# Gated scan with eight decay blocks: levels built on tokens, a plain product on the diagonal, key products in three pieces

## The reference, cut to what matters

```python
def step(s, inp):                       # one chunk of tokens, one head, one direction
    qc, kc, vc, gc = (t.astype(F32) for t in inp)
    g = jnp.cumsum(gc, axis=2)
    diff = g[:, :, :, None, :] - g[:, :, None, :, :]
    decay = jnp.exp(jnp.where(mask, diff, -jnp.inf))
    att = jnp.einsum('bhik,bhjk,bhijk->bhij', qc, kc, decay)
    o = jnp.einsum('bhij,bhjv->bhiv', att, vc) + jnp.einsum('bhik,bhkv->bhiv', qc * jnp.exp(g), s)
    g_last = g[:, :, -1:, :]
    s = s * jnp.exp(g_last[:, :, 0, :, None]) + jnp.einsum('bhjk,bhjv->bhkv', kc * jnp.exp(g_last - g), vc)
    return s, o
```

## Time and profile before

| | before |
|---|---|
| median of the runs | 3596.71 us |
| profiled execution | 3596.57 us |
| its span on the core | 3594.8 us |
| TensorE busy / share | 3305.3 us / 92% |
| VectorE busy / share | 2276.3 us / 63% |
| GpSimd busy / share | 1000.4 us / 28% |
| L815 key products | 80 of 2660 ns, 212.8 us |
| L1057 predicated copies | 320 of 298 ns |

### The profile page before, as it was taken

How to read it: one execution, slowest core, us unless ns; L and a number is a source line. 1 busy time by engine, 2 the same in 40 slices (tenths; PEclk the granted TensorE clock), 3 DMA queues, 4 the chain that set the end, 5 groups by cost and what they waited for, 6 DMA issues and landing times. The chain is left out here.

```text
span 3594.8 us, 49981 instructions
## 1 busy us (share of the span) xinstructions
PE 3305.3 (92%) x18422; PEld 2780.7 (77%) x18422; DVE 2276.3 (63%) x2915; ACT 993.8 (28%) x1472; POOL 1000.4 (28%) x539
## 2 busy tenths in 40 slices
PE   5989999997979999999997879888988799999998
PEld 3889978886868888888885657777777688888886
DVE  7976078888356666666666256666664556666666
ACT  4111245545141111111112434444442311112111
POOL 1322155552232222222220131212121333333331
PEclk8999999998989999999998879999999899999999
DMA  5557110002211111111100200000002111111111
GB/s 200 188 181 281 61 67 1 1 1 84 82 60 36 35 35 42 40 35 41 35 29 12 72 9 5 6 5 5 6 13 77 42 59 47 41 53 52 47 41 59
DMA packets 64253, 196.27 MB, mean 55 GB/s; under 512 B 7680, under 2 KB 20864, under 8 KB 62848
## 3 DMA queue, kind: packets, MB, share of 16 engines
q1 hardware_dynamic: 47280, 163.96, 13.8%
q10 hardware_dynamic: 16848, 30.56, 2.5%
HBM read 175.62 MB, written 18.87 MB: 54 GB/s over the span
## 5 line engine op out<-in xcount | busy, mean ns | idle before, releaser
L1407 DVE SCALAR_TENSOR_TENSOR resid<-ps,mod,resid 128x512 f32<-128x512 f32 (+1 forms) x880 | 601.6, 697 | 473.7 <-PE ps L1303 473.4
L1310 PE MATMUL ps<-hf_hi,up_hi 128*128 128x512 f32 (+1 forms) x1760 | 653.3, 371 | 31.6 <-DVE hf_lo L285 22.6
L1310 PE MATMUL ps<-hf_lo,up_hi 128*128 128x512 f32 (+1 forms) x1760 | 652.5, 371 | 0.0
L1310 PE MATMUL ps<-hf_hi,up_lo 128*128 128x512 f32 (+1 forms) x1760 | 650.9, 370 | 0.0
L1278 POOL TENSOR_SCALAR up_hi<-up_raw 128x1024 fp32r<-128x1024 f32 x88 | 94.5, 1074 | 1162.7 <-PE ps L1310 1101.0
L1310 PEld LDWEIGHTS ps<-hf_hi,up_hi 128*128 128x128 f32 x1760 | 335.2, 190 | 88.4 <-issue 34.8
L1310 PEld LDWEIGHTS ps<-hf_hi,up_lo 128*128 128x128 f32 x1760 | 334.3, 190 | 56.4
L1310 PEld LDWEIGHTS ps<-hf_lo,up_hi 128*128 128x128 f32 x1760 | 335.2, 190 | 51.7
L1303 PE MATMUL ps<-act_hi,dn_hi 128*128 128x512 f32 (+1 forms) x880 | 332.9, 378 | 18.6 <-DVE act_lo L1428 16.1
L1359 ACT ACTIVATE conv<-ps,conv_w 128x1280 f32<-128x1280 f32 (+1 forms) x88 | 115.7, 1314 | 803.9 <-PE ps L1310 803.6
L1303 PE MATMUL ps<-act_lo,dn_hi 128*128 128x512 f32 (+1 forms) x880 | 326.7, 371 | 0.0
(11 more groups left out here) (239 smaller groups left out, 6902.5 us busy)
## 6 DMA issues: line engine op xcount, KB each, us to landing
up_raw<-in_up SPq DMA_DIRECT2D x88, 512.0 KB, 3.6
adaw_ring<-in_adaw SPq DMA_DIRECT2D x80, 512.0 KB, 4.2
dn_raw<-in_dn SPq DMA_DIRECT2D x44, 512.0 KB, 3.6
vr<-vr_out ACTq DMA_DIRECT2D x80, 128.0 KB, 2.7
adaw_first<-in_adaw SPq DMA_DIRECT2D x16, 512.0 KB, 22.0
wvr_raw<-in_wvr SPq DMA_DIRECT2D x8, 1024.0 KB, 6.7
x<-in_xT ACTq DMA_DIRECT2D x8, 640.0 KB, 16.8
r<-vr ACTq DMA_DIRECT2D x10, 512.0 KB, 3.8
```

The costliest lines, as they stand in the source:

```text
L1310: mm = pe.matmul(c.psf[:, at:at + w], a[:, half, k, :], b[:, k, t:t + w], start=(k == 0 and a is up_hi and b is h_hi), stop=(k == KD - 1 a ...
L1407: dve.scalar_tensor_tensor(resid[:, m, t:t + w], c.ps[:, 6 + j % 2, 0:w], c.mod[:, gate + m, cond[t]:cond[t] + 1], resid[:, m, t:t + w], A ...
```

## The change

Before, the 9 decayed blocks are three coarse levels, three quarter blocks and pairs for groups of 16 and 4, and a last level of two. Now the tree has six plain levels (sizes 128 down to 4), whose middle is a token (that token counts as a key and as a query), so that the level of two is not needed: odd neighbours are covered by the levels above, and even tokens take their own diagonal element from the undecayed product of key and query. One more element, the pair of the last two tokens, comes from the remaining-decay block by a product with one column (now L886). `NBLK` is 8 instead of 10, `NQUERY` 7 instead of 6, `NKEY` 7 instead of 9, `PICKS` 5 instead of 4. GpSimd makes the key product in three instructions, of 3, 2 and 2 blocks. The transpose is a function of its own, `turn`, behind decay and gate; it writes the same bank of `ps` as the diagonal product and so waits until VectorE has made the first of its five copies, the one of the diagonal.

```diff
-CUM, LEVEL, QUARTERS, PAIRS, QUARTER2, QUARTER3, LAST, REST = 0, 1, 4, 5, 6, 7, 8, 9
-NBLK = 10
-NQUERY, NKEY = 6, 9
-PICKS = 4
+LEVELS = 6
+CUM, LEVEL, REST = 0, 1, 1 + LEVELS
+NBLK = 2 + LEVELS
+NQUERY, NKEY = 1 + LEVELS, 1 + LEVELS
+PICKS = 1 + LEVELS - COARSE + 1
+PARTS = (0, 3, 5, NKEY)
+KPARTS = len(PARTS) - 1
...
-    E_PS, TURN_PS, TREE_PS, O_PS, KS_PS, GATE_PS = 0, 2 * BANK + 256, 3 * BANK, 5 * BANK, 6 * BANK, 7 * BANK
+    E_PS, TREE_PS, DIAG_PS, O_PS, KS_PS, GATE_PS = 0, 2 * BANK, 4 * BANK, 5 * BANK, 6 * BANK, 7 * BANK
+    TURN_PS = DIAG_PS + P
...
-                    pool.tensor_tensor(
-                        kd[u % 2][:, :].rearrange("p (b t) -> p b t", t=P),
-                        e[:, u % 2, LEVEL * P:NBLK * P].rearrange("p (b t) -> p b t", t=P),
-                        qk[:, GH + h, bass.ds(chunk[d] * P, P)].unsqueeze(1).broadcast_to([P, NKEY, P]),
-                        ALU.mult).then_inc(k_set, 1)
+                    for lo, hi in zip(PARTS, PARTS[1:]):
+                        pool.tensor_tensor(
+                            kd[u % 2][:, lo * P:hi * P].rearrange("p (b t) -> p b t", t=P),
+                            e[:, u % 2, (LEVEL + lo) * P:(LEVEL + hi) * P].rearrange("p (b t) -> p b t", t=P),
+                            qk[:, GH + h, bass.ds(chunk[d] * P, P)].unsqueeze(1).broadcast_to([P, hi - lo, P]),
+                            ALU.mult).then_inc(k_set, 1)
...
                 for t in range(0, NBLK * P, BANK):
-                    m = min(BANK, NBLK * P - t)
-                    if m < BANK and (u >= 2 or not begins(s)):
-                        pe.wait_ge(kt_set, s * U + (u - 1))
...
                 for b in range(COARSE):
                     size = P >> b
                     half = size // 2
                     for k0 in range(0, P, size):
-                        left, right = (k0, k0 + half) if d == 0 else (k0 + half, k0)
+                        r0, r1 = mirrored(k0, k0 + half)
+                        c0, c1 = mirrored(k0 + half - 1, k0 + size - 1 + (k0 + size == P))
...
-                own = qd[:, u % 4, QUARTERS * P:(QUARTERS + 1) * P]
-                for n, block in ((1, QUARTERS), (2, QUARTER2), (3, QUARTER3)):
-                    level(1, keys(block), own, 16, 4, n)
-                level(2, keys(PAIRS), qd[:, u % 4, PAIRS * P:(PAIRS + 1) * P], 4, 2, 1)
-                level(3, keys(LAST), query[:, 0, :], 2, 2, 1)
-                level(3, key[:, 0, :], query[:, 0, :], 2, 2, 0).then_inc(tree_done, 1)
-                pe.wait_ge(kt_set, s * U + u)
-                pe.wait_ge(e_set, s * U + (u + (1 if ends(s) and u == U - 1 else 2)))
-                pe.transpose(c.psf[:, TURN_PS:TURN_PS + P], kd[u % 2][:, (REST - LEVEL) * P:NKEY * P],
-                             c.ident[:, :]).then_inc(turned, 1)
+                for b in range(COARSE, LEVELS):
+                    level(at + (b - COARSE + 1) * P, keys(LEVEL + b), queries(LEVEL + b))
+                if not (begins(s) and u == 0):
+                    pe.wait_ge(picked, s * (U * PICKS) + ((u - 1) * PICKS + 1))
+                pe.wait_ge(kt_set, s * U + u)
+                level(DIAG_PS, key, query)
+                r0, c0 = (P - 32, P - 1) if d == 0 else (0, 0)
+                pe.matmul(c.psf[r0:r0 + 32, DIAG_PS + c0:DIAG_PS + c0 + 1], keys(REST)[:, r0:r0 + 32],
+                          query[:, c0:c0 + 1], start=True, stop=True).then_inc(tree_done, 1)
+
+            def turn(s, u):
+                pe.wait_ge(picked, s * (U * PICKS) + (u * PICKS + 1))
+                pe.transpose(c.psf[:, TURN_PS:TURN_PS + P], kd[u % 2][:, (REST - LEVEL) * P:NKEY * P], c.ident[:, :]).then_inc(turned, 1)
...
                         gate(s + 1, u // 4)
+                    turn(s, u)
                     if u:
                         output(s, u - 1, chunk)
```

More of the change, by code:

```diff
@@ L840, in decay @@
                 for t in range(0, NBLK * P, BANK):
-                    m = min(BANK, NBLK * P - t)
-                    if m < BANK and (u >= 2 or not begins(s)):
-                        pe.wait_ge(kt_set, s * U + (u - 1))
                     for n, a in enumerate((lg_hi, lg_lo)):
-                        mm = pe.matmul(c.psf[:, E_PS + t:E_PS + t + m], a[:, d, h * P:(h + 1) * P],
-                                       tree[:, d, t:t + m], start=(n == 0), stop=(n == 1))
+                        mm = pe.matmul(c.psf[:, E_PS + t:E_PS + t + BANK], a[:, d, h * P:(h + 1) * P],
+                                       tree[:, d, t:t + BANK], start=(n == 0), stop=(n == 1))
                 mm.then_inc(e_done, 1)
@@ L851, in products @@
                 raw = slice(h, h + 1), slice(GH + h, GH + h + 1)
-                query, key = (qk[:, at, bass.ds(chunk[d] * P, P)] for at in raw)
+                query, key = (qk[:, at, bass.ds(chunk[d] * P, P)][:, 0, :] for at in raw)
                 pe.wait_ge(q_set, s * U + (u + 1))
-                pe.wait_ge(k_set, s * U + (u + 1))
+                pe.wait_ge(k_set, s * (U * KPARTS) + (u + 1) * KPARTS)
                 at = TREE_PS + u % 2 * BANK
@@ L858, in keys, with queries, mirrored, level @@
                     return kd[u % 2][:, (block - LEVEL) * P:(block - LEVEL + 1) * P]
[L860 to L867, removed]
+                def queries(block):
+                    return qd[:, u % 4, block * P:(block + 1) * P]
+                def mirrored(a, b):
+                    return (a, b) if d == 0 else (P - b, P - a)
+                def level(to, key, query):
+                    pe.matmul(c.psf[:, to:to + P], key, query, start=True, stop=True)
                 for b in range(COARSE):
@@ L888, in products @@
-                pe.transpose(c.psf[:, TURN_PS:TURN_PS + P], kd[u % 2][:, (REST - LEVEL) * P:NKEY * P],
-                             c.ident[:, :]).then_inc(turned, 1)
+                        r0, r1 = mirrored(k0, k0 + half)
+                        c0, c1 = mirrored(k0 + half - 1, k0 + size - 1 + (k0 + size == P))
+                        r0 -= r0 % 32
+                        pe.matmul(c.psf[r0:r1, at + c0:at + c1], keys(LEVEL + b)[:, r0:r1],
+                                  queries(LEVEL + b)[:, c0:c1], start=True, stop=True)
@@ L978, in decay @@
                     act.wait_ge(fade_set, s * U + (u - 1))
-                    act.wait_ge(k_set, s * U + (u - 1))
+                    act.wait_ge(k_set, s * (U * KPARTS) + (u - 1) * KPARTS)
                 act.activation(e[:, u % 2, :], c.psf[:, E_PS:E_PS + NBLK * P], ACT.Exp,
@@ L1056, in attention @@
                     dve.wait_ge(picked, (s * U + u) * PICKS + n)
+                    pick = (n - 1) % PICKS
+                    source = DIAG_PS if n == 0 else at + pick * P
                     mm = dve.copy_predicated(
-                        att[:, d, u % 2, :], mask[:, d, n * P:(n + 1) * P].bitcast(mybir.dt.int32),
-                        c.psf[:, at + n * P:at + (n + 1) * P])
+                        att[:, d, u % 2, :], mask[:, d, pick * P:(pick + 1) * P].bitcast(mybir.dt.int32),
+                        c.psf[:, source:source + P])
                     mm.then_inc(picked, 1)
@@ L2167, in tree_constants @@
     mask = np.zeros((2, P, PICKS, P), np.float32)
-    def between(low, high):
-        return (t[:, None] > low) & (t[:, None] <= high)
-    def same(size):
-        return t[:, None] // size == t[None] // size
-    for block, size in ((LEVEL, 128), (LEVEL + 1, 64), (LEVEL + 2, 32), (PAIRS, 4), (LAST, 2)):
-        middle = t // size * size + size // 2 - 1
-        low, high = np.minimum(t, middle), np.maximum(t, middle)
-        tree[0, :, block, :] = between(low, high)
-        pick = 0 if size > 4 else 2 if size == 4 else 3
-        mask[0, :, pick, :] += same(size) & (t[:, None] <= middle[:, None]) & (t[None] > middle[None])
-    tree[0, :, LAST, :] = between(t, t // 2 * 2 + 1)
-    mask[0, :, 3, :] += np.eye(P)
-    quarter = t % 16 // 4
-    mask[0, :, 1, :] = same(16) & (quarter[:, None] < quarter[None])
-    for block, n in ((QUARTERS, 1), (QUARTER2, 2), (QUARTER3, 3)):
-        edge = t // 16 * 16 + 4 * n - 1
-        tree[0, :, block, :] = between(t, edge) & (quarter < n)
-    own = t // 4 * 4 - 1
-    tree[0, :, QUARTERS, :] += between(own, t) & (quarter > 0)
+    for level in range(LEVELS):
+        size = P >> level
+        edge = t // size * size + size // 2 - 1
+        low, high = np.minimum(t, edge), np.maximum(t, edge)
+        tree[0, :, LEVEL + level, :] = (t[:, None] > low) & (t[:, None] <= high)
+        mask[0, :, max(level - COARSE + 1, 0), :] += ((t[:, None] // size == t[None] // size)
+                                                      & (t[:, None] <= edge[:, None]) & (t[None] >= edge[None])
+                                                      & ((t[None] % size < size - 1) | (t[None] == P - 1)))
+    mask[0, :, PICKS - 1, :] = (t[:, None] == t[None]) & ((t[None] % 2 == 0) | (t[None] == P - 1))
+    mask[0, P - 2, PICKS - 1, P - 1] = 1
     tree[0, :, CUM, :] = t[:, None] <= t[None]
```

## The result

The changed kernel takes 3604.80 us, the median of nine runs (3603.66 to 3607.69), against 3595.12 us of the kernel before in nine runs (3593.14 to 3597.22). The ratio is 1.0026 with a 95% interval of 1.0016 to 1.0036: slower by 0.26%. 3585 had been forecast, faster by 0.3%, with a range up to 3613, so the time lies in the range and the direction is wrong.

What follows compares the result with a forecast made beforehand. TensorE was taken to bound the scan. Groups of four units at 18.89 against 19.34 us gave -8.1 and the last step -4.4, together -12.5: 3584, rounded to 3585 us, range 3560 to 3613.

Steps and rivals of the forecast that it cites:

- What bounds the kernel now: Scan stage before the change: TensorE works 383.35 of 385.00 us; VectorE's queries wait for the port at no cost.
- TensorE's own work: TensorE per unit after the change: 4.00 us instead of 4.55, worth 44 us over 80 units if nothing else counted.
- extra one-column product: TensorE's added product for the last two tokens: two small instructions at 0.035 each, 0.07 us per unit.
- products to decay 1.5 us: Sign expected in the profile after: TensorE takes 1.5 us from its products to decay.
- The new wait: Transpose waits for VectorE's first copy, closing a loop through ScalarE, GpSimd and VectorE: 3.96 us in a plain unit.
- fade 0.18 later, the exp 0.09 later: ScalarE links in the loop after the copy of the turned keys, putting the exp 0.58 us behind the transpose's start.
- The port between two pieces: A waiting VectorE query gets the shared port between two GpSimd key pieces, then takes 0.87 us.
- The sum: Scan stage: four units take 18.89 us against 19.34; 18 groups and the last step give -12.5 us.
- The third: Rival: the loop is some tenths longer per unit from dearer pieces or semaphores, 3597 to 3606 us; 18%.
- The first: Rival: TensorE alone decides the scan, 44 us go, 3553 us; half way 3568; together 15%.
- The second: Rival: GpSimd keeps the port through its three key pieces, making the loop 5.30 us, 3636 us; 9%.
- the fourth: Rival: TensorE's full-width products pay weight load and columns one after the other, 3655 us; 2%.

Runs made afterwards that it cites:

- e8: The kernel before with its key product in three instructions of 384 columns: 3596.02 us, ratio 1.0000 to before.
- e4: The changed kernel without the one-column product, leaving out the attention element of a chunk's last two tokens: 3598.65 us, ratio 1.0010 to before.
- e9: The changed kernel, transpose's wait kept, with the diagonal product first and the one-column product beside the coarse levels: 3593.61 us, ratio 0.9991 to before.
- e1: The changed kernel with the transpose's target in another bank, so it no longer waits for VectorE's first copy: 3570.56 us, ratio 0.9931 to before.
- e2: The changed kernel with the transpose in another bank and also ahead of decay: 3566.28 us, ratio 0.9919 to before.
- e10: The changed kernel with the transpose's wait for the first copy kept, but the transpose ahead of decay and gate: 3663.40 us, ratio 1.0185 to before.
- e7: The changed kernel with transpose in another bank and ahead of decay, diagonal product first, one-column product beside coarse levels: 3546.77 us, ratio 0.9860 to before.
- e5: The changed kernel with the key product in one instruction of 896 columns instead of three: 3620.70 us, ratio 1.0067 to before.

## Why the prediction was wrong

**What bounds the kernel now** was right: TensorE in the scan, VectorE with slack of a unit, queries that wait for the port. e8 shows the slack: shorter waits bring nothing.

**TensorE's own work, "Sum 4.00 us, 0.55 less than 4.55"**: this failed in size. A plain unit is 4.27 us (step 9), so that the saving is 0.28 us, 22 us in all instead of 44. The step that failed is the "extra one-column product: 2 x 0.035 = 0.07". I took the price of small products among small products for that of a small one between full-width ones. e4 shows the term: without it a unit that TensorE rules is 0.35 us shorter, 4.32 to 3.97, and 3.97 is within 0.04 of the sum without that term. In the row of after, the full-width pair at 645.17 (0.22) is followed by decay at 645.64, 0.25 for the two small instructions; the other 0.1 is that decay in e4 starts 0.14 behind the pair's start, ahead of the 0.22 that the pair takes. e9 shows the same size by moving it. The full-width products were right to 0.06 a unit: six instructions from 644.40 to 645.17 and the pair's 0.22 make 0.99 where 0.93 was reckoned. So of the signs named ahead, "products to decay 1.5 us" failed, with 1.74 (643.90 to 645.64).

**The new wait** was named, and its loop as well, link by link. Two links were too short: "fade 0.18 later, the exp 0.09 later". The exp writes the buffer that fade reads and waits for fade to end, so it starts 0.38 us behind fade's start (642.88 to 643.26, and the row of ScalarE's exp waiting for its own fade, 59 times). Before, that wait was hidden behind the one for decay (0.79 in the earlier trace rows). And the copy of the turned keys comes 0.37, not 0.31, behind. So the exp starts at 0.92 instead of 0.58 and the key product at 2.12 (2.00 in other turns) instead of 1.77, and the terms behind them are late: in most steps 5.5 to 5.7 us with `gate_sum` where 5.30 was reckoned, and 4.9 to 5.1 with `gate_low` where 4.45 was. Plain units don't lose by it. In some the query asks ahead of the key product, which I had not thought of:

```profile
654.94 1.09 DVE L1045 TENSOR_TENSOR q_decayed<-decay,qk 128x896 f32<-128x896 f32 x1
...
655.11 3.17 POOL L820 TENSOR_TENSOR k_decayed<-decay,qk 128x384 f32<-128x384 f32 x3 [2.35 <-ACT decay L983]
...
656.93 0.39 PE L847 MATMUL ps<-tree,lg_lo 128*128 128x512 f32 x1
...
657.16 0.27 PE L891 MATMUL ps<-ident,k_decayed 128*128 128x128 f32 x1
```

The query at 654.94 is 0.17 us ahead of the key product, and the transpose at 657.16 follows decay by 0.23 with no wait. In the others it comes just behind the first piece and waits for that piece alone, as reckoned; such a loop takes 4.21 us (e4) where 3.96 was reckoned, still less than TensorE's 4.27.

**The port between two pieces** was right:

```profile
547.03 3.23 POOL L820 TENSOR_TENSOR k_decayed<-decay,qk 128x384 f32<-128x384 f32 x3 [1.69 <-ACT decay L983]
...
547.09 1.88 DVE L1045 TENSOR_TENSOR q_decayed<-decay,qk 128x896 f32<-128x896 f32 x1
```

The query asked 0.06 us behind the first piece and ended at 548.97, 0.95 us behind the end of that piece (548.02 with the 0.99 reckoned for it), with two pieces of GpSimd's three still to come. One figure that this rested on was not: L2038 alone takes 0.68 us, the median of its 16, and not 0.53; it ended 0.55 behind the GpSimd instruction all the same.

**The sum.** A group of four units (from one gate matmul to the next) was reckoned at 18.89 us. It is 5.47 + 4.32 + 5.55 + 4.91 = 20.25 in step 1, and 20.1 in the mean of steps 1 to 8, against 19.43 before. Of the 1.36 missing in step 1, 0.65 are TensorE's in two units, 0.25 and 0.46 the loop's in the other two. Over 18 groups and the last step, TensorE's error alone takes the forecast of -12.5 us to about +1 and the loop's alone to about 0; together they turned the sign.

**The rivals.** The third (a loop longer by some tenths, 3597 to 3606) comes nearest, with 18%, and that its time fits is in part luck: it puts the whole loss on the loop, and about half of it is TensorE's own work. I gave it no mechanism beyond dearer pieces and semaphores, though ScalarE's order against buffers was there to be read. The first, TensorE alone, is what e1 and e2 make of the kernel. The second, GpSimd holding the port, and the fourth, load and columns in series, did not occur. The Trainium skill ("TensorE: Matmul & The Clock Gate", Part 3, The mechanism) has a weight load overlap with a running matmul only when the row group differs. By that rule the eight instructions from 644.40 would need 1.76 us, an estimate at 0.22 each, and they take 1.09: the trace doesn't agree.

**What stays open**: why a small product between full-width ones costs 0.35 us. Its weight load starts at 645.48, 0.12 us behind the end of the load before, where the loads of the full-width products follow each other without a gap; no run here tells whether the load, the change of tile or the emptying of the array sets the time.

## What to carry to other kernels

When a change puts two results into one bank, ask who reads the one and who waits to write the other: slack of a whole unit was lost to such a wait, at 34 us, and another bank gave it back. Reckon a new loop with every link's true release, a buffer's last reader on the same engine included, and price a small matmul by its neighbours. A step that a queue must wait for belongs behind work that doesn't depend on it: e10 puts it ahead and pays. A small product belongs among other small ones.

## What the runs showed of the hardware that was not expected

- A small tile between full-width products: 32 rows and one column, two instructions, cost 0.25 us in the row and 0.35 by leaving them out (e4), and nothing that shows among other small ones (e7: 16 small instructions in 0.49 us, as long as 14 took before; e9: the distances of e4 to 0.03 us).
- The clock: in e10, waits of up to 1.9 us on TensorE came with stretches at granted clock 0.50, among them 645 to 648 us, and output products at half speed in them; in after, with waits of up to 1.23 us, it stayed at 1.00 from 500 to 800 us.
- The port goes to whoever asks first, and between two pieces to the one that waits. In e5 the query that asked 0.07 us ahead ended 1.08 us later, and one that came behind waited for the whole product. A program whose two engines ask at nearly the same time has units of two lengths: the distance from unit 4, which holds `gate_low`, is 4.42 us in step 7, where the query starts 0.01 us ahead of the second piece, and 4.90 in step 1, where it starts 0.09 behind it.
